# Forgetting attention's queries and keys turned by VectorE and a trip through memory, and the inverse's diagonal blocks placed in both orientations

## Time and profile before

| | |
|---|---|
| median of three runs | 1134.5 us (1133.76 to 1135.17) |
| the profiled execution | 1133.93 us |
| its span, first to last instruction | 1132.0 us |
| TensorE busy | 1123.1 us, 99% |
| VectorE, ScalarE, GpSimd busy | 756.8, 588.0, 108.0 us |
| mean granted TensorE clock | 0.999 |

### The profile page before, as it was taken

The page is one execution under the profiler, slowest core; times in us unless marked ns, Lnnn a source line. Parts: engine busy times, 40 slices in busy tenths (PEclk is TensorE's granted clock), DMA queues, the critical chain, the costliest instruction groups (busy, mean ns, idle before and its releaser), DMA issues.

```text
span 1132.0 us, 15919 instructions
## 1 busy us (share of the span) xinstructions
PE 1123.1 (99%) x6129; PEld 973.1 (86%) x6129; DVE 756.8 (67%) x965; ACT 588.0 (52%) x782; POOL 108.0 (10%) x161
## 2 busy tenths in 40 slices
PE   9999999999999999999999999999999999999997
PEld 8998888888889999988888888888888888888886
DVE  6866687657876887863666564566867566655566
ACT  6765654446465765642554444454654365444453
POOL 6410211000011000000000000200500020000011
PEclk9999999999999999999999999999999999999999
DMA  8743753565644766565488866477856669876642
GB/s 259 204 158 98 226 188 113 167 204 173 218 135 145 235 208 187 176 207 186 156 276 255 246 204 220 146 255 234 256 187 203 225 201 292 242 245 220 213 141 75
DMA packets 129589, 225.78 MB, mean 199 GB/s; under 512 B 12161, under 2 KB 58866, under 8 KB 129523
## 3 DMA queue, kind: packets, MB, share of 16 engines
q1 hardware_dynamic: 125921, 214.37, 59.6%
q10 hardware_dynamic: 3506, 10.49, 2.7%
q0 software_dynamic: 96, 0.01, 0.1%
HBM read 215.80 MB, written 9.04 MB: 199 GB/s over the span
## 4 chain that ended last, share of the span: by engine, by line
PE 93%; DVE 3%; DMA 1%; issue 1%; ACT 1%; POOL 0%; POOLq 0%; DVEq 0%; SPq 0%; ACTq 0%
PE ACCP L918 28%; PE ACCP L920 28%; PE ACCP L919 28%; PE SMP L1135 3%; DVE CONVF L2367 1%; DVE LO L2238 1%; PE SMP L1128 1%; DMA RAW<-in_w_in_dram 1%; DMA X<-in_x_dram 0%; PE SMP L1302 0%; PE SMP L1286 0%; PE SMP L1082 0%; PE SMP L1088 0%; PE SMP L1083 0%; PE SMP L1470 0%
## 5 line engine op out<-in xcount | busy, mean ns | idle before, releaser
L2238 DVE TENSOR_TENSOR LO<-RAW,HI 128x1024 fp32r<-128x1024 f32 x365 | 438.9, 1240 | 209.8 <-ACT HI L1656 205.1
L1656 ACT ACTIVATE HI<-RAW 128x1024 fp32r<-128x1024 f32 x366 | 370.5, 1054 | 274.3 <-PE ACCP L920 232.6
L918 PE MATMUL ACCP<-HI,XH 128*128 128x512 f32 (+1 forms) x776 | 303.2, 391 | 0.0
L920 PE MATMUL ACCP<-HI,XL 128*128 128x512 f32 (+1 forms) x776 | 300.6, 387 | 0.0
L919 PE MATMUL ACCP<-LO,XH 128*128 128x512 f32 (+1 forms) x776 | 300.3, 387 | 0.0
L920 PEld LDWEIGHTS ACCP<-HI,XL 128*128 128x128 f32 x776 | 145.7, 188 | 30.1
L919 PEld LDWEIGHTS ACCP<-LO,XH 128*128 128x128 f32 x776 | 145.8, 188 | 28.7
L918 PEld LDWEIGHTS ACCP<-HI,XH 128*128 128x128 f32 x776 | 145.8, 188 | 28.7
L918 PE MATMUL ACCP<-XH,HI 128*128 128x256 f32 x512 | 145.4, 284 | 0.4 <-DVE CONVF L2367 0.4
L920 PE MATMUL ACCP<-XH,LO 128*128 128x256 f32 x512 | 144.9, 283 | 0.0
L919 PE MATMUL ACCP<-XL,HI 128*128 128x256 f32 x512 | 144.9, 283 | 0.0
(11 more groups left out here) (409 smaller groups left out, 1133.1 us busy)
## 6 DMA issues: line engine op xcount, KB each, us to landing
RAW<-in_w_in_dram SPq DMA_DIRECT2D x104, 512.0 KB, 4.6
RAW<-in_w_up_dram SPq DMA_DIRECT2D x44, 512.0 KB, 4.5
RAW<-in_ffn_w_gate_dram SPq DMA_DIRECT2D x44, 512.0 KB, 4.6
RAW<-in_ffn_w_up_dram SPq DMA_DIRECT2D x44, 512.0 KB, 4.6
RAW<-in_ffn_w_down_dram SPq DMA_DIRECT2D x44, 512.0 KB, 4.1
RAW<-in_w_down_dram SPq DMA_DIRECT2D x22, 512.0 KB, 4.0
scratch_hidden<-TURNED SPq DMA_DIRECT2D x10, 512.0 KB, 5.6
BLOCKS<-scratch_hidden SPq DMA_DIRECT2D x40, 128.0 KB, 4.0
```

Of the source, the lines that this page charges most:

```text
L918: pe.matmul(dst, lhs[0], rhs[0], start=start, stop=False)
L920: return pe.matmul(dst, lhs[1], rhs[0], start=False, stop=stop)
L1656: act.activation(HI[:, n % RING, half_of(half)], RAW[:, n % RAWS, half, :], ACT.Copy).then_inc(hi_ready, 1)
L2238: dve.tensor_tensor(LO[:, s, c], RAW[:, n % RAWS, half, :], HI[:, s, c].bitcast(f32), ALU.subtract).then_inc(lo_ready[s], 1)
```

## The change

The 24 transpositions by PE and the copies out of PSUM go. The solved diagonal blocks are copied by DVE into the other orientation (DIAG_ROWS), stored by SP, and placed in ME by eight DMAs behind the load of block 21; POOL first clears ME. Queries and keys are transposed in 32x32 squares by DVE (four instructions of 128x512 into FOX_TURNED), stored in memory by two DMAs of 512 KB ahead of the load of block 23, and read back by eight DMAs of 128 KB behind that load and ahead of block 24's; ACT then copies them into FQK with the gain, in four instructions, ahead of its HI of block 24. Its copy of Z16_0 is moved ahead of those. DVE's FMASK is moved behind the turn and block 21. PE waits for the second placing in `joined(16)` and for `fox_taken` before `fox_scores`. Six names leave SMALL; every later name keeps its distance of four to the one it follows in its bank, but moves by two banks.

```diff
@@ -149,7 +149,7 @@
 MIX_TURNS = [(t, b) for b in range(2) for t in range(NT)]
 SMALL = [f"norm_mix.{t}{b}" for t, b in MIX_TURNS] + ["cols0", "cols1", "cols2", "tinyT", "tiny"]
 SMALL += ["gTq0", "gTq1", "gTk0", "gTk1", "gTv0", "gTv1", "gcol", "grow0", "grow1", "gFk0", "gFk1"]
-SMALL += ["kk0", "kk1", "kq0", "kq1", "z0", "z1", "z2", "z3", "rc0", "rc1", "rc2", "rc3", "so0", "so1", "T16_0", "T16_1", "fTq0", "fTq1", "fTk0", "fTk1"]
+SMALL += ["kk0", "kk1", "kq0", "kq1", "z0", "z1", "z2", "z3", "rc0", "rc1", "rc2", "rc3", "so0", "so1"]
 SMALL += ["Z16_0", "Z16_1", "Tt32_0", "Tt32_1", "fS0", "fS1a", "fS1b", "Z32_0", "Z32_1", "T32_0", "T32_1"]
 SMALL += ["Tt64_0", "Tt64_1", "fP0", "fP1a", "fP1b", "fo0", "fo1", "Z64_0", "Z64_1", "T64_0", "T64_1"]
 SMALL += ["Tt128_0", "Tt128_1", "vn0", "S1", "kS", "qS", "vn1", "o0", "o1", "yT0", "yT1"]
@@ -279,7 +279,8 @@
 
 
         DIAG_L, DIAG_T, DIAG_TERM = (at(f"diag_{n}", 40 + i, [N_DIAG, 16, 16]) for i, n in enumerate(["L", "T", "term"]))
-        diag_l, diag_t = (nc.dram_tensor(f"scratch_diag_{n}", (NT * HEADS, P // 16, 16, 16), f32) for n in "lt")
+        DIAG_ROWS = at("DIAG_ROWS", 43, [N_DIAG, 16, 16])
+        diag_l, diag_t, diag_rows = (nc.dram_tensor(f"scratch_diag_{n}", (NT * HEADS, P // 16, 16, 16), f32) for n in ("l", "t", "rows"))
         GSQ = at("GSQ", 32, [P, NT, 2 * HW])
         OSQ = at("OSQ", 32, [P, NT, HW])
         DO = at("DO", 40, [P, NT, HW])
@@ -290,6 +291,8 @@
         SP_ = at("SP_", 70, [P, HEADS, 384])
         FV = at("FV", 76, [P, NT, HW])
         FQK = at("FQK", 64, [P, 2 * HEADS, SEQ])
+        FOX_TURNED = [at(f"FOX_TURNED{i}", 52 + 4 * i, [P, 4, NT, 4, 32]) for i in range(2)]
+        fox_rows = [nc.dram_tensor(f"scratch_fox{i}", (4, 32, 4, NT * 128), f32) for i in range(2)]
         FP0 = at("FP0", 52, [P, HEADS, P])
         FP1 = at("FP1", 54, [P, HEADS, SEQ])
         FPT0 = at("FPT0", 58, [P, HEADS, P])
@@ -398,6 +401,8 @@
         heads_sq, heads_sums, heads_ready, root_ready = sems("heads_sq heads_sums heads_ready root_ready")
         rates_ready, rates_exp, decay_args, decay_ready, level_ready = sems("rates_ready rates_exp decay_args decay_ready level_ready")
         rhs_ready = sem("rhs_ready")
+        fox_turned, fox_taken, diag_rows_solved, diag_rows_stored, diag_rows_placed = sems("fox_turned fox_taken diag_rows_solved diag_rows_stored diag_rows_placed")
+        fox_out, fox_in = ([sem(f"fox_{n}{i}") for i in range(2)] for n in ("out", "in"))
         keep_abs, keep_ln, keep_ready, stick_ready = sems("keep_abs keep_ln keep_ready stick_ready")
         row_max, probs_ready = sems("row_max probs_ready")
         y_hi = sem("y_hi")
@@ -694,6 +699,8 @@
             sp.dma_start(DIAG_L[:, :, :].rearrange("b r c -> b (r c)"), diag_l[:, :, :, :].rearrange("q g r c -> (q g) (r c)")).then_inc(diag_loaded, 16)
             sp.wait_ge(diag_solved, 1)
             sp.dma_start(diag_t[:, :, :, :].rearrange("q g c r -> (q g) (c r)"), DIAG_T[:, :, :].rearrange("b c r -> b (c r)")).then_inc(diag_stored, 16)
+            sp.wait_ge(diag_rows_solved, 1)
+            sp.dma_start(diag_rows[:, :, :, :].rearrange("q g r c -> (q g) (r c)"), DIAG_ROWS[:, :, :].rearrange("b r c -> b (r c)")).then_inc(diag_rows_stored, 16)
             for g, branch, wo in (("c", 2, "w_oc"), ("a", 0, "w_oa"), ("b", 1, "w_ob")):
                 if g == "b":
                     load_t("gz", w["w_in"], C_GZ)
@@ -704,8 +711,24 @@
                         sp.wait_ge(diag_zeroed, 3)
                         for i in range(P // 16):
                             sp.dma_start(diagonal(MP, i), diag_t[:, i, :, :].rearrange("q c r -> c q r")).then_inc(diag_placed, 16)
+                    if g == "c" and j == 3:
+                        sp.wait_ge(diag_rows_stored, 16)
+                        sp.wait_ge(diag_zeroed, 4)
+                        for i in range(P // 16):
+                            sp.dma_start(diagonal(ME, i), diag_rows[:, i, :, :].rearrange("q r c -> r q c")).then_inc(diag_rows_placed, 16)
                 for j in range(2):
+                    if g == "c" and j == 1:
+                        for i in range(2):
+                            sp.wait_ge(fox_turned, NT * (i + 1))
+                            sp.dma_start(fox_rows[i][:, :, :, :].rearrange("b f q c -> (b f) (q c)"),
+                                         FOX_TURNED[i][:, :, :, :, :].rearrange("p q m k t -> p (q m k t)")).then_inc(fox_out[i], 16)
                     load(f"out_{g}", Turn(j), rows(w[wo], 0, 4, 512 * j, 512))
+                    if g == "c" and j == 1:
+                        for i in range(2):
+                            sp.wait_ge(fox_out[i], 16)
+                            for q in range(4):
+                                sp.dma_start(FOX_TURNED[i][32 * q:32 * q + 32].rearrange("p b m k t -> p b (m k t)"),
+                                             fox_rows[i][:, :, q, :].rearrange("b f c -> f b c")).then_inc(fox_in[i], 16)
             load_d("w_out", w["w_out"])
             load_t("mem_k", w["w_mkv"], 0)
             load_t("mem_q", w["w_mq"], 0)
@@ -863,6 +886,7 @@
             pool.memset(DIAG_T[:, :, :], 0.0).then_inc(diag_zeroed, 1)
             pool.wait_ge(diag_zeroed, 2)
             pool.memset(DIAG_T[:, :, :].rearrange("b c r -> b (c r)")[:, 0:256:17], 1.0).then_inc(diag_zeroed, 1)
+            pool.memset(ME[:, :, :, :], 0.0).then_inc(diag_zeroed, 1)
 
             lo_of(ON_POOL_CONV)
             heads_root(0, 1.0)
@@ -1267,14 +1291,7 @@
                     last = pe.matmul(dst[:, P:SEQ], SV[:, 1, h * P:(h + 1) * P], Z[:, h, SEQ:SEQ + P], start=False, stop=True)
                 finish(last)
             t_half("gate_c", 0, XH, XL)
-            pe.wait_ge(diag_placed, 16 * (P // 16))
-            for t in range(NT):
-                turn_four(f"T16_{t}", lambda h: MP[:, t, h, :])
             t_half("gate_c", 1, XH, XL)
-            for i, part in enumerate("qk"):
-                for t in range(NT):
-                    pe.wait_ge(heads_ready, 2 + t + 1)
-                    turn_four(f"fT{part}{t}", lambda h: HT[:, t, i * HW + h * P:i * HW + (h + 1) * P])
 
             def join(b, n):
 
@@ -1295,7 +1312,10 @@
 
                 for t in range(NT):
                     small_is_taken(pe, f"Z{b}_{t}")
-                    small_is_taken(pe, f"T{b}_{t}")
+                    if b > 16:
+                        small_is_taken(pe, f"T{b}_{t}")
+                    else:
+                        pe.wait_ge(diag_rows_placed, 16 * (P // 16))
                     name, m = f"Tt{2 * b}_{t}", P - b
                     small_bank_free(pe, name)
                     for h in range(HEADS):
@@ -1303,6 +1323,7 @@
                     finish(last)
 
             t_half("gate_c", 2, XH, XL)
+            pe.wait_ge(diag_placed, 16 * (P // 16))
             join(16, 0)
             t_half("gate_c", 3, XH, XL)
             joined(16)
@@ -1316,9 +1337,7 @@
             o_gemm("out_c", 0, y_is_ready("so0", "so1"))
 
 
-            for part in "qk":
-                for t in range(NT):
-                    small_is_taken(pe, f"fT{part}{t}")
+            pe.wait_ge(fox_taken, 2 * NT)
 
             def fox_scores(name, t, heads):
                 small_bank_free(pe, name)
@@ -1828,14 +1847,16 @@
             act.wait_ge(diag_stored, 16)
             gate_bias_load("c")
             gate_bias_load("a")
-            take_small("T16_0", ME[:, 0], by_head(small("T16_0")))
             split_ahead("gate_c", Turn(0))
-            take_small("fTq0", FQK[:, 0:4, tok(0)], by_head(small("fTq0")), col("fox_qnorm"))
-            take_small("fTk0", FQK[:, 4:8, tok(0)], by_head(small("fTk0")), col("fox_knorm"))
             gates("c", 0)
             split_ahead("gate_c", Turn(1))
+            take_small("Z16_0", MB[0:112, 0, :, 0:64], by_head(small("Z16_0")[0:112, 0:256], 64))
+            for i, gain in enumerate(("fox_qnorm", "fox_knorm")):
+                act.wait_ge(fox_in[i], 64)
+                for m in range(NT):
+                    copy(FQK[:, 4 * i:4 * i + 4, tok(m)].rearrange("p k (b t) -> p k b t", b=4),
+                         FOX_TURNED[i][:, :, m].rearrange("p b k t -> p k b t"), fox_taken, col(gain))
             split_ahead("gate_c", Turn(2))
-            take_small("Z16_0", MB[0:112, 0, :, 0:64], by_head(small("Z16_0")[0:112, 0:256], 64))
             gates("c", 1)
             split_ahead("gate_c", Turn(3))
             split_ahead("out_c", Turn(0))
@@ -2445,6 +2466,8 @@
                 if j < 14:
                     link(ins)
             ins.then_inc(diag_solved, 1)
+            dve.wait_ge(diag_solved, 1)
+            dve.tensor_copy(DIAG_ROWS[:, :, :], DIAG_T[:, :, :].rearrange("b c r -> b r c")).then_inc(diag_rows_solved, 1)
             split_ahead("foxqk", Turn(0))
             split_ahead("foxqk", Turn(1))
 
@@ -2470,15 +2493,15 @@
```

(12 more changed lines are left out.)

## The result

| | before | after |
|---|---|---|
| median of five runs each | 1134.79 us (1133.76 to 1135.55) | 1141.24 us (1139.42 to 1141.55) |
| ratio after to before | | 1.0055, 95% interval 1.004 to 1.0069 |
| the profiled execution | 1133.93 us | 1141.31 us |
| its span | 1132.0 us | 1139.6 us |
| mean granted TensorE clock | 0.999 | 0.994 |

The changed kernel is slower, by 6.5 us in the medians and 7.4 us in the profiled executions; 1138.3 with a range of 1135.0 to 1141.5 was forecast. The direction and the place are the forecast's, and so is the mechanism in the main: a copy that waits, by way of other engines, for late transfers. The size is at the range's far end, and the terms behind it are to be gone through.

What follows compares the result with a forecast made beforehand. TensorE, busy 99% of the span, was taken to bound the kernel. Terms of -2.6 (transpositions), +5.2 (stall) and +1.2 (clock) gave +3.8 on 1133.93, 1137.7; with the median 0.57 above that execution, 1138.3 us, range 1135.0 to 1141.5.

Steps and rivals of the forecast that it cites:

- What bounds the kernel: Whole kernel: TensorE, busy 99% of the span; the copy of Z16_1 for `joined(16)` is just in time, without slack.
- (1): TensorE before `joined(16)`: its transpositions go, 2.6 us less, all on the path.
- (2): Diagonal blocks in the second orientation: 0.4 us passes through the loads to `heads_scale`; nothing reaches TensorE at once.
- (3): VectorE from `heads_scale` to the gate's bias: with four transpositions, the bias begins at 151.4, 0.9 us later.
- (4): ScalarE's gates and block 23's HI: Z16_0 is copied at 155.1 to 155.5, early enough.
- (5): Trip of queries and keys through memory: out 5.6, back 4.0, load 6.0 us; block 24 lands at 159.6 and 160.5.
- (6): Second half of `joined(16)`: waits for Z16_1 behind block 24, a stall of 5.2 us, bounds 3.1 to 7.2.
- (7): TensorE's clock after the stall: half rate costs between 0 and 2.4 us; 1.2 taken.
- the model trip: The feed-forward trip through memory, taken as having the same sizes: out 5.6 us, four issues in 1.76 us.
- the wait for RAW: Sign of being right: ScalarE waits for a DMA into RAW ahead of block 24's HI.
- slow trip and cold clock: Rival, 10%: stores, loads and returns slow each other; stall 7.2, clock 2.4, net +7.0, 1141.5 us.
- No stall: Rival, 6%: block 24's LO is done before Z16_1's copy is wanted, so the 2.6 us stay gained: 1131.9.
- does not do what it says: Rival, 3%: the slowest wait was another, and little changes: 1134.5 us.

Runs made afterwards that it cites:

- the repeat: The changed kernel run once more without any edit, beside a kernel before at 1134.09: 1139.93 us (1139.0 to 1142.65).
- the load first: Changed kernel with ScalarE's HI of block 24 ahead of its four copies and SP issuing block 24's load ahead of the returns: 1135.42 us, ratio 1.0008.
- the best version: Changed kernel with VectorE's copy of Z16_1, gate's bias and subtraction of join(32) moved ahead of block 24's LO: 1131.29 us, ratio 0.9974.
- large pieces: Changed kernel with returns reading memory in written order, pieces of 4 KB instead of 1 KB, turn left unfinished: 1139.76 us (1139.43 to 1139.82).

## Why the prediction came out as it did

- **What bounds the kernel, and (1)**: right. 2.6 us are to be had of TensorE, and only if Z16_1 is copied earlier and the subtraction of join(32) with it. The version with VectorE's order changed gets them.
- **(2)**: too low. The undoing of this part alone does not take the loss away, but VectorE's transpositions began at 143.98, 0.8 us later than step (3) had them, and at 142.65 with this part undone: what comes through is nearer to 1.3 us than to the 0.4 that I had let through.
- **(3), (4)**: VectorE's steps right to a microsecond, though three copies of turned results had gone from it and not two; ScalarE's copy of Z16_0 began at 157.2 and not 155.1, since block 23's second half landed late as well. It ended at 157.54 and so held the first half of `joined(16)` by some 0.2 us, to 157.60; the stop behind it swallowed that, and the queries came back later still.
- **(5), the term that was mis-sized.** "I take the middle, because the model trip has the same sizes, order and queue, and here a second store of 512 KB stands in it." The issue times were right within a microsecond, the landings wrong both ways: out 2.7 for 5.6, back 6.0 (8.9 the last) for 4.0, block 24 9.6 for 6.0. The model trip moves half as much, and the middle value counted the second trip's issues on SP but not its bytes through the shared engines; those stand only among the rivals. The run with quartered returns shows that the bytes matter: with 0.75 MB less, block 24 lands in 4.8. They are not the whole of it, since with all the bytes it landed anywhere from 5.8 to 10.2 us from one profile to another.
- **(6)**: right from HI of block 24 on; ahead of it ScalarE waited for the keys and not, as forecast, for block 24, and the one hid the other. Only in the two runs with HI ahead of the copies does the trace show the wait for RAW that the prediction named as a sign. The stop was 7.9 and not 5.2, beyond the upper bound of 7.2. That bound took the longest landing of the model's stretch, 8.0, as a ceiling; a ceiling read in a stretch with less traffic is none.
- **(7)**: 1.9 us in the profiled execution, between 1.2 and the upper end of 2.4, but 3.0 in the repeat, beyond that end. In the trace the granted clock fell to 0.50 during the stop of 7.9 us, and the distance of the matmuls doubled behind it. The rule cited there (the Trainium skill, "TensorE: Matmul & The Clock Gate", section "HAM oscillation — how this bites in real kernels") agrees: a wait for transfers made the cold price due again. I should have taken it at its full price, since shorter stops than the one I forecast already bring most of it: those of 2.9 and 3.6 us cost 1.7. The reading behind the 2.4 is weaker than it looked: the profile gives a granted clock of 1.00 for the kernel's first 8 us, so the slow instructions there are half as fast without a row that puts it on the clock; behind the stop the row itself says 0.50.
- **The rivals**: *slow trip and cold clock* described this execution best: 7.2 and 2.4 for 7.9 and 1.9. Given 10%, it deserved more. That the time lay in the range is partly luck: the range reached out to that rival, the median is 0.3 us inside its upper end, and one of the five runs, 1141.55, lies beyond it. My own middle, +3.8, was 2.6 us short of the measured +6.45. *No stall* and *does not do what it says* are excluded by the rows.
- **What remains open**: why the engines move 209 to 248 GB/s at full share while returns are under way and 391 behind them. Piece size explains little of it. That the returns read what has just been written was not tried, nor was sending them from another engine's queue than SP's. Nor is it known why the landings differ so much between executions with the same transfers, or why the cold clock cost 1.7 us in some and 3.0 in others.

## What to carry to other kernels

An engine's cheap step that releases a faster engine must not stand in program order behind a step that waits for a transfer: move it first, then judge the change that makes the transfer late. Here the same 24 transpositions taken out cost 6.5 us or gave 3.4, by three steps of VectorE's order. When a trip through memory is added, count its bytes against every load issued behind it, not only its issues; and when a stop of some microseconds arises on TensorE, add the cold clock to it, here 1.7 to 3.0 us.

## What the runs showed of the hardware

- Behind stops of 2.9 to 8.5 us TensorE's granted clock was at 0.50 in every profile, and the price does not follow the length of the stop: 1.7 us behind 2.9 and 3.6, 3.0 behind 3.9 and 8.5, 1.9 behind 6.4 and 7.9.
- Behind a short stop the fall can show only after the work has begun again: with quartered returns (stop 3.6) the granted clock was 1.00 up to 163.0 and then 0.52 and 0.63; the second half took 1.17 us there and 1.75 behind 7.9. One minus the granted clock, over those stretches, gives (0.48 + 0.37) x 2 = 1.7 us. With the diagonal blocks undone (stop 3.9) it had fallen before the work began, and the second half took 1.76.
- The outward stores of 512 KB landed in 2.6 to 2.8 us in every profile with the trip, where those of the feed-forward trip took 5.6.
- Runs of one kernel scatter by different amounts: the changed one's five in the repeat lie 3.6 us apart, the ten with the load first 5.0, the nine of the best version 1.4, but four with large pieces only 0.4. Part of it is the clock: of the 1.3 us between the changed kernel's two profiled executions, 1.1 lie in its price, 1.9 against 3.0.
